# A two-block transformer step on one core: the first block's gates and branch products computed with tokens in partitions, the merged activations transposed between and inside fills

## What is computed

```python
xn = rms_norm(h, norm1_g)
proj = xn @ w_in                      # q, k, v, qi, ki, wi, su, sv, ga, gb
y_attn = dsa_attention(q, k, v, qi, ki, wi)          # 8 heads, top 64 keys
y_sgu = spatial_gating(gelu(su), gelu(sv), ...)
merged = (sigmoid(ga) * (y_sgu @ w_branch_a)
          + sigmoid(gb) * (y_attn @ w_branch_b))     # 256 x 1024
h = h + merged @ w_out
h = h + hier_moe(rms_norm(h, norm2_g), ...)          # 32 experts, 96 MB of weights
```

## Time and profile before

| | before |
|---|---|
| median of three runs | 905.92 us |
| the profiled execution | 905.84 us |
| its span, first to last instruction | 904.1 us |
| mean granted clock of TensorE | 0.98 |
| busy: TensorE, VectorE, ScalarE, GpSimd | 832.4, 494.7, 377.9, 87.2 us |
| bytes moved, mean rate | 217.51 MB, 241 GB/s |

### The profile page before, as it was taken

The page is one execution under the profiler, slowest core; times in us unless marked ns, Lnnn a source line. Parts: engine busy times, 40 slices in busy tenths (PEclk is TensorE's granted clock), DMA queues, the critical chain, the costliest instruction groups (busy, mean ns, idle before and its releaser), DMA issues.

```text
span 904.1 us, 13983 instructions
## 1 busy us (share of the span) xinstructions
PE 832.4 (92%) x5603; PEld 673.2 (74%) x5603; DVE 494.7 (55%) x771; ACT 377.9 (42%) x520; POOL 87.2 (10%) x111
## 2 busy tenths in 40 slices
PE   5989999999999987866698899999999899999996
PEld 4989789989998633322332699877778799999995
DVE  5899577854564511100110576565675577667584
ACT  5333454465334211001011665456544466556452
POOL 4122000111000000000000101122160000000000
PEclk9999999999999999988899999999999999999999
DMA  8665556225778999999999995534627447546511
GB/s 278 232 197 188 187 180 238 96 94 187 266 290 346 420 420 422 422 422 421 422 422 404 322 208 187 180 114 173 179 102 248 148 143 249 166 156 232 169 47 47
DMA packets 95292, 217.51 MB, mean 241 GB/s; under 512 B 14031, under 2 KB 44877, under 8 KB 83465
## 3 DMA queue, kind: packets, MB, share of 16 engines
q1 hardware_dynamic: 94553, 215.33, 65.7%
q10 hardware_dynamic: 576, 1.18, 0.4%
q0 software_dynamic: 112, 0.30, 0.3%
HBM read 215.44 MB, written 1.34 MB: 240 GB/s over the span
## 4 chain that ended last, share of the span: by engine, by line
PE 70%; DMA 12%; DVE 10%; ACT 4%; issue 2%; SPq 1%; POOL 1%; DVEq 0%; ACTq 0%
PE ps L909 16%; PE ps L911 16%; PE ps L910 16%; DMA moe_ring<-in_w_expert_in 10%; PE ps L1391 6%; PE ps L1295 6%; DVE w_lo L1781 3%; PE ps L1260 1%; PE ps L1321 1%; PE ps L1315 1%; DMA stage<-in_w_in 1%; PE ps L1101 1%; PE ps L1111 1%; DMA h_tok<-in_x 1%; ACT w_odd L1472 1%
## 5 line engine op out<-in xcount | busy, mean ns | idle before, releaser
L911 PE MATMUL ps<-x_hi,w_lo 128*128 128x256 f32 x568 | 162.3, 286 | 0.0
L1781 DVE TENSOR_TENSOR w_lo<-stage,w_hi 128x2048 fp32r<-128x2048 f32 (+1 forms) x44 | 101.9, 2354 | 25.3 <-ACT w_hi L1472 23.7
L911 PEld LDWEIGHTS ps<-x_hi,w_lo 128*128 128x128 f32 x568 | 110.8, 195 | 0.0
L909 PE MATMUL ps<-x_hi,w_hi 128*128 128x256 f32 x360 | 105.0, 292 | 3.8 <-DVE w_lo L1781 3.0
L910 PE MATMUL ps<-x_lo,w_hi 128*128 128x256 f32 x360 | 103.6, 288 | 0.0
L1472 ACT ACTIVATE w_hi<-stage 128x2048 fp32r<-128x2048 f32 (+1 forms) x44 | 79.2, 1849 | 55.3 <-PE ps L911 49.7
L909 PEld LDWEIGHTS ps<-x_hi,w_hi 128*128 128x128 f32 x360 | 70.9, 197 | 4.7 <-issue 2.9
L910 PEld LDWEIGHTS ps<-x_lo,w_hi 128*128 128x128 f32 x360 | 71.0, 197 | 0.1
L910 PE MATMUL ps<-w_lo,x_hi 128*128 128x512 f32 (+1 forms) x168 | 63.8, 380 | 0.0
L909 PE MATMUL ps<-x_hi,w_odd 128*128 128x256 f32 x216 | 61.4, 284 | 1.3 <-DVE x_lo L1767 1.3
L910 PE MATMUL ps<-x_lo,w_odd 128*128 128x256 f32 x216 | 61.1, 283 | 0.0
(11 more groups left out here) (394 smaller groups left out, 2038.0 us busy)
## 6 DMA issues: line engine op xcount, KB each, us to landing
stage<-in_w_in SPq DMA_DIRECT2D x23, 2048.0 KB, 7.9
moe_ring<-in_w_expert_in SPq DMA_DIRECT2D x38, 1024.0 KB, 18.2
moe_ring<-in_w_expert_out SPq DMA_DIRECT2D x16, 1024.0 KB, 17.5
stage_b<-in_w_up SPq DMA_DIRECT2D x12, 1024.0 KB, 7.7
stage<-in_w_down SPq DMA_DIRECT2D x11, 1024.0 KB, 5.1
stage<-in_w_up SPq DMA_DIRECT2D x10, 1024.0 KB, 8.8
up_odd<-in_w_expert_in SPq DMA_DIRECT2D x8, 1024.0 KB, 18.3
down_odd_a<-in_w_expert_out SPq DMA_DIRECT2D x6, 1024.0 KB, 24.5
```

What stands on the lines that cost most here:

```text
L909: mm(out, still[0], moving[0], start=first, stop=False)
L911: return mm(out, still[1], moving[0], start=False, stop=last)
L1781: tt(lo[:, cols], staged(n)[:, cols], hi[:, cols].bitcast(fp32), ALU.subtract).then_inc(lo_ready, 1)
```

## The change

All sixteen fills of ga, gb, wa and wb go by tokens: 24 matmuls of 512 columns instead of 48 of 256. Gates, products and `merged` then have tokens in partitions (`ga_tok`, `sv_tok`, `xs_tok`). Since wo needs features in partitions for its stationary operand, four steps `mw` transpose `merged`, four tiles of 128 x 128 each, into PSUM; ScalarE copies the high half into `x_hi`, VectorE subtracts for `x_lo`; the splits of `merged` go. mw 0 stands behind wb 1, mw 1 behind wb 2, mw 2 behind wb 3, and mw 3 inside wo 0, behind its sixth k. ScalarE's wait for the fourth mix moves from ga 2 to ga 1. SP's list is unchanged.

```diff
@@ schedule @@
+    fills = []
     for name in ("wa", "wb"):
         for u in range(2):
-            steps.extend(unit(name, u, [2 * u, 2 * u + 1]))
+            fills += unit(name, u, [2 * u, 2 * u + 1])
+    steps.extend(fills[0:6])
+    at("mw", 0)
+    steps.append(fills[6])
+    at("mw", 1)
+    steps.append(fills[7])
+    at("mw", 2)
+    at("mw", 3)
+    steps[-1]["inside"] = ("wo", 0)
     steps.extend(unit("wo", 0, [0, 1]))
...
@@ TensorE, fills @@
-                if kind == "wo" and i == 0:
-                    for k in range(0, KT, 2):
-                        coming.append((k, lambda k=k: eng.wait_ge(dve_split, 4 + k // 2 + 1)))
+                if kind == "wo" and i < 2:
+                    for u in range(2):
+                        coming.append((u * KT // 2, lambda u=u: wait_read(eng, "at", "mw", 2 * u + i)))
...
-                elif kind in ("qi", "q", "k", "su", "ga", "gb", "qka", "qc"):
+                elif kind in ("qi", "q", "k", "su", "qka", "qc"):
...
-                elif kind in ("v", "sv", "g2"):
+                elif kind in ("v", "sv", "ga", "gb", "g2"):
                     last = by_tokens(bank, 0, BANK, i % 2, w, 0)
                 elif kind == "wa":
                     if i == 0:
                         eng.wait_ge(dve_split, 4)
-                    for m in range(2):
-                        last = by_features(bank, m * S, w, ((i % 2) * 2 + m) * P, x=(ys_hi, ys_lo))
+                    last = by_tokens(bank, 0, BANK, i % 2, w, 0, x=(ys_hi, ys_lo))
                 elif kind == "wb":
...
+                    last = by_tokens(bank, 0, BANK, i % 2, w, 0, x=(ya_hi, ya_lo))
...
-                elif (kind, i) == ("wo2", 0):
+                elif kind in ("wo", "wo2") and i == 0:
                     by_tokens(bank, 0, BANK, 0, w, 0, ks=range(0, 6))
                     for inner in steps:
-                        if inner.get("inside"):
+                        if inner.get("inside") == (kind, 0):
                             fill_at(inner)
                     last = by_tokens(bank, 0, BANK, 0, w, 0, ks=range(6, KT))
...
+                elif kind == "mw":
+                    eng.wait_ge(merged_ready, i + 1)
+                    for kk in range(4):
+                        c = (4 * (i // 2) + kk) * P
+                        last = eng.transpose(ps[:, bank, kk * P:(kk + 1) * P], xs_tok[:, i % 2, c:c + P], ident[:, :])
@@ ScalarE @@
                 elif kind == "ga":
-                    if i == 2:
+                    if i == 1:
                         eng.wait_ge(mixed, 4)
-                    act(gate_ga[:, 2 * i:2 * i + 2, :], two, ACT.Tanh, scale=0.5).then_inc(free, 1)
+                    act(ga_tok[:, i % 2, i // 2 * BANK:(i // 2 + 1) * BANK], src, ACT.Tanh, scale=0.5).then_inc(free, 1)
...
-                elif kind == "wb":
-                    eng.wait_ge(merged_ready, i + 1)
-                    split_tiles(x_hi, merged, 2 * i)
...
-                elif kind == "mt":
+                elif kind in ("mw", "mt"):
                     eng.wait_ge(at_full, n + 1)
-                    t, u = i // 2, i % 2
+                    u, t = (i // 2, i % 2) if kind == "mw" else (i % 2, i // 2)
                     act(x_hi[:, 4 * u:4 * u + 4, t * P:(t + 1) * P], src.rearrange("p (k c) -> p k c", k=4), ACT.Copy).then_inc(mt_hi, 1)
@@ VectorE @@
-                    for tiles in ([j - 1] if j > 0 else []) + ([3] if j == 3 else []):
-                        split_tiles(x_lo, merged, x_hi, 2 * tiles)
...
-                elif kind == "mt":
-                    eng.wait_ge(mt_hi, i + 1)
-                    to = (slice(4 * (i % 2), 4 * (i % 2) + 4), slice(i // 2 * P, i // 2 * P + P))
+                elif kind in ("mw", "mt"):
+                    u, t = (i // 2, i % 2) if kind == "mw" else (i % 2, i // 2)
+                    eng.wait_ge(mt_hi, i + (1 if kind == "mw" else 5))
+                    to = (slice(4 * u, 4 * u + 4), slice(t * P, t * P + P))
```

More of the change, by code:

```diff
@@ L231, in schedule @@
         at("mt", i)
-        steps[-1]["inside"] = True
+        steps[-1]["inside"] = ("wo2", 0)
     steps.extend(unit("wo2", 0, [0, 1]))
@@ L348, in two_blocks @@
         sv_tok = sv[:, :].rearrange("p (t d) -> p t d", t=NT)
-        gate_sv = sv[:, :].rearrange("p (f t) -> p f t", t=S)
         down_hi = at_kib("down_hi", 152, [P, 2 * D], r32)
@@ L365, in two_blocks @@
         junk = mreg[:, :].rearrange("p (t d) -> p t d", t=NT)
-        merged = mreg[:, :].rearrange("p (f t) -> p f t", t=S)
         rope_a = mreg[:, 0:2 * BANK].rearrange("p (b n) -> p b n", b=2)
@@ L976, in fill_pj @@
                         wait_read(eng, "at", "av", HEADS - 1)
-                    for m in range(2):
-                        last = by_features(bank, m * S, w, ((i % 2) * 2 + m) * P, x=(ya_hi, ya_lo))
+                    last = by_tokens(bank, 0, BANK, i % 2, w, 0, x=(ya_hi, ya_lo))
                 elif (kind, i) == ("wo", 3):
                     last = wo_last(range(9, 3 * KT))
-                elif (kind, i) == ("wo2", 0):
+                elif kind in ("wo", "wo2") and i == 0:
                     by_tokens(bank, 0, BANK, 0, w, 0, ks=range(0, 6))
                     for inner in steps:
-                        if inner.get("inside"):
+                        if inner.get("inside") == (kind, 0):
                             fill_at(inner)
@@ L1503, in evac_pj @@
                         eng.wait_ge(at_full, where["mix", 3] + 1)
-                    act(gate_sv[:, 2 * i:2 * i + 2, :], two, ACT.Tanh, scale=0.5).then_inc(free, 1)
+                    act(sv_tok[:, i % 2, i // 2 * BANK:(i // 2 + 1) * BANK], src, ACT.Tanh, scale=0.5).then_inc(free, 1)
                 elif kind == "g2":
@@ L1871, in evac_pj @@
                         wait_read(eng, "pj", *(("gb", 3) if kind == "wa" else ("g2", 7)))
-                    if kind == "wa":
-                        out, g, new = merged[:, 2 * i:2 * i + 2, :], gate_ga[:, 2 * i:2 * i + 2, :], two
-                    else:
-                        t, c = i // 4, (i // 2) % 2 * BANK
-                        out, g, new = merged2[:, t, c:c + BANK], su_tok[:, t, c:c + BANK], src
-                    stt(out, g, 1.0, new, ALU.add, ALU.mult).then_inc(free, 1)
+                    t, c = (i % 2, i // 2 * BANK) if kind == "wa" else (i // 4, (i // 2) % 2 * BANK)
+                    out, g = (xs_tok, ga_tok) if kind == "wa" else (merged2, su_tok)
+                    stt(out[:, t, c:c + BANK], g[:, t, c:c + BANK], 1.0, src, ALU.add, ALU.mult).then_inc(free, 1)
                 elif kind in ("wb", "pab", "pc"):
@@ L1882, in evac_pj @@
                         wait_read(eng, "pj", "g2", 11)
-                    if kind == "wb":
-                        part = slice(2 * j, 2 * j + 2)
-                        m, g, new = merged[:, part, :], gate_sv[:, part, :], two
-                    else:
-                        t, c = j // 2, j % 2 * BANK
-                        m, g, new = merged2[:, t, c:c + BANK], (ga_tok if kind == "pc" else sv_tok)[:, t, c:c + BANK], src
-                    step(stt(g, g, 1.0, new, ALU.add, ALU.mult))
+                    t, c = (j % 2, j // 2 * BANK) if kind == "wb" else (j // 2, j % 2 * BANK)
+                    m, g = (xs_tok if kind == "wb" else merged2), (ga_tok if kind == "pc" else sv_tok)
+                    m, g = m[:, t, c:c + BANK], g[:, t, c:c + BANK]
+                    step(stt(g, g, 1.0, src, ALU.add, ALU.mult))
                     eng.sem_inc(free, 1)
@@ L1897, in evac_pj @@
                     eng.sem_inc(merged_ready, 1)
-                    if kind == "pc":
-                        return
-                    for tiles in ([j - 1] if j > 0 else []) + ([3] if j == 3 else []):
-                        split_tiles(x_lo, merged, x_hi, 2 * tiles)
                 elif kind in ("wo", "wo2"):
```

## The result

The changed kernel takes 908.7 us (median of 13 runs, 906.55 to 911.76), the kernel before 906.18 (13 runs beside them, 904.93 to 907.61): ratio 1.0031, 95% interval 1.0023 to 1.0039. Slower by 0.3%; the forecast was 907.2 and most likely no change that can be measured. The time lies inside the forecast's range (904.4 to 908.9), but that it is measurably slower had a chance of only 0.30. One run of the repetition further down took 1181.59 us at a mean granted clock of 0.66; it is in none of the medians.

The account below looks back on a forecast made before the run. Bound: the DMA stream of expert weights, started by the end of VectorE's last wo split. That end moves 1.33 us later although TensorE is 1.60 us earlier; 905.84 plus 1.33 gives 907.2 us, range 904.4 to 908.9.

Parts of the forecast that it names:

- D: End of VectorE's split of the last wo unit, which starts the expert weight stream: 278.87 to 280.20, 1.33 us later.
- The wait for ptb: TensorE's waits for ScalarE's copy of ptb in 158 to 192 us: longer by about 0.3 us a head.
- gb: Its four wide fills under attention: 0.66 us gained of a possible 1.13, limited by GpSimd's last scaling ahead of pt 7.
- The transposes: Sixteen new ones in four groups at 0.44 us a group: three ahead of wo, 1.32 us, and one inside it.
- Rival C: Transposes among fills not overlapped, exposing 0.27 us each: first wo matmul later, 909.7 us; chance 0.10.
- rival D: A wide fill with activations as weights is no shorter than a narrow one: 910.1 us; chance 0.05.
- C's line of 0.17 us a transpose: Cost of one transpose among the fills from which on Rival C was said to decide.
- Behind D, one for one: Expert weight stream: same bytes, always full, so it and the second block start 1.33 us later, as D does.
- the 20.20 us at 339.72: Expert stage: TensorE said to stand 20.20 us on a load issued at 339.72, as evidence of a full queue.
- The second block has no changed instruction: Second block: its chain was to be shifted by 1.3 us and otherwise equal, with no further cost.
- The median of the runs is 0.08 above the profiled one, so the two may be used alike: Kernel before: median 905.92 against profiled 905.84 us, so the sum on the profile was taken as the median's forecast.
- the line of 0.2%: Whole kernel: about 1.8 us, the smallest difference that a measurement was taken to tell from no change.

Follow-up runs that it names:

- the repetition: The changed kernel run again, unaltered, for a second profile: 908.85 us, 1.0031 of the kernel before.
- the late split: The kernel before with one more VectorE subtraction (128 x 1408) ahead of the second step of the last wo unit's split: 908.10 us, 1.0024.
- the split ahead: The changed kernel with the copy of the fourth group of transposes moved behind the two splits of the last wo unit: 905.44 us, 0.9995.
- the mended kernel: The changed kernel with the fourth group behind the last wo unit's splits and TensorE's waits at ga and the second block's norm filled: 904.34 us, 0.9986.
- the last kernel: The mended kernel with 48 small transposes (8 x 8) at its start, while TensorE waits for its first load: 904.19 us, 0.9979.
- neither filling alone: The changed kernel with unread TensorE work in one wait: ahead of the ga fills 908.51 us, 1.0031; in the second block's norm 908.65 us, 1.0023.

## Why the prediction failed

*D: right.* Predicted later by 1.33 us, through mw 3's copy ahead of ScalarE's split; measured 1.19 against the work at 144 us. The numbers on the way, each shifted by the 0.93 us by which this execution is ahead: first wa matmul 223.32 (predicted 223.28), first wo matmul 268.28 (268.49), fourth group 272.50 (272.60), copy 273.13 (273.24), ScalarE's split 273.63 (273.78), VectorE's 275.57 (275.71), D 280.06 (280.20). The wait for ptb grew by 0.26 to 0.27 us at each of three heads, as said, and up to the first wa matmul the changed kernel gains 0.62 us (78.64 us behind the split at 144, from 79.26), where 0.66 were forecast for gb.

*The transposes: right.* 272 ns by themselves, 0.35 us a group of four from its first to the next product (271.57 to 271.92); I had 0.44. Rival C falls, and with it rival D, the wide form that is no shorter: the first wa and the first wo matmul are where the sum put them. (C's line of 0.17 us a transpose doesn't follow from its own terms: with 16 x 0.03 = 0.48 above + 1.33 the time passes + 1.8 us at 0.14.)

*Behind D, one for one: right.* D to vvf 222.58 against 222.61, and the late split shows it by itself. In the other direction it holds only in part: of the 3.4 us by which D comes earlier with the split ahead 1.3 reach vvf, and 2.3 in the mended kernel (144 to vvf 355.48 and 354.55 us, against 356.80), since the stream then runs low near 310 us. One reading on the way was wrong: the 20.20 us at 339.72 are the load's time from issue to landing, and TensorE's own wait for it is 5.1 us. That the queue was full doesn't hang on it.

*"The second block has no changed instruction": true, and the wrong conclusion.* I took it as shifted and otherwise equal. It lost 0.50 us (0.6 in the repetition) on the w_up load, because 368 matmuls fewer move TensorE's instruction transfers. This term was put at nothing without a reason, and the trace of before would have shown the risk: the transfer stood at 693.1 us, 1.0 us behind the end of the wait.

*"The median of the runs is 0.08 above the profiled one, so the two may be used alike": this is the step that failed.* It holds for before, where 31 of 33 runs lie within 2 us (its one profile has the fall in 44 to 70 us and no other). It does not hold for the changed kernel: in 11 of its 13 runs the time is 1.5 to 5.2 us above the one that was profiled. From the profiles, one fall costs 0.9 (44 to 70 us), 1.5 (near 193), 1.3 to 2.4 (near 711). On common ground, with the first of them in both, the profiled executions would be 905.8 and 907.5; the medians are 906.2 and 908.7. So of the 2.5 us between the medians 1.2 are D and 0.5 the instruction transfer; the remaining 0.8 I put down to the falls of the clock. That is argued, not shown: the six profiled executions above 908 us all have a fall near 193 or near 711, and the eight below 907.5 have none, but neither filling alone moved the median clear of the changed kernel's.

The forecast of 907.2 was thus short by 1.5 us. With the instruction transfer's 0.5 it would have stood at 907.7, just at the line of 0.2%; what goes beyond that, most likely the falls of the clock, carried the kernel over it. With a forecast of +1.33 us and a line at 1.8, a quarter of the chance above the line was too little: 625 us of trace behind D stood in the sum without any term, and without an uncertainty of their own.

**What stays open.** Why the clock falls in one execution and not in the next, and why it rarely does in before: the delay alone brings the upper times, the wide gates alone bring them, and executions that idle as long keep the clock at either place. Where the other 0.6 of the 2.10 us behind a D at 275 go. And why the short w_up wait of the last kernel brings 0.1 us and not 0.5.

## What to carry to other kernels

When a step moves into an engine's ordered list, look at what is queued behind it and which transfer that releases: a group of four transposes that takes TensorE 0.35 us made the kernel's transfers start 1.2 us later, and their place in the list was worth 3.4 us of the median. A kernel that runs an instruction transfer about every 120 matmuls has no untouched part: fewer instructions early can move those transfers into other loads late, which here cost 0.2 to 0.7 us for one on the path; look in the trace of before for transfers that stand next to a load on the chain. And before a small change is judged by medians, list the runs: two clusters 1.5 to 2.5 us apart can mean that the clock or a collision comes and goes, and a filled wait is a cheap thing to try against the first.

## What was not expected of the hardware

The granted clock fell to 1.2 GHz inside a kernel whose TensorE is 91% busy, behind idle stretches of 1.3 to 2.7 us, for some us, in some executions of the same program and not in others; one such fall costs 0.9 to 2.4 us. A single 16 KB instruction transfer, about 1.1 us on one of the 16 DMA engines, lengthened ScalarE's wait for a 2 x 1 MB load from 3.9 to 5.4 us (5.0 in one kernel, with less of the time lost). 48 transposes of 8 x 8 take 1.34 us, 28 ns each.
